# Rope's inverse roots, convolution taps and context sums at new places in a two-block transformer kernel

## What is computed

```python
def mixer(h, ...):
    qa, ka, va, ub, qc, kc, vc, gates = jnp.split(h @ w_in, IN_SPLITS, axis=-1)
    qa = apply_rope(rms_norm(qa.reshape(B, S, 2 * DA_HEADS, DA_HEAD_DIM), qn_g), cos, sin)
    ka = apply_rope(rms_norm(ka.reshape(B, S, 2 * DA_HEADS, DA_HEAD_DIM), kn_g), cos, sin)
    y_a = diff_attention(qa, ka, va, lam, lambda_init, subln_g) @ w_proj_a
    y_b = conformer_conv(ub, w_dw, b_dw, conv_ln_g, conv_ln_b) @ w_proj_b + b_proj_b
    y_c = stick_breaking(qc, kc, vc) @ w_proj_c
    g = jax.nn.sigmoid(gates.reshape(B, S, N_BRANCH, D_MODEL))
    return (g[:, :, 0] * y_a + g[:, :, 1] * y_b + g[:, :, 2] * y_c) @ w_out

def rms_norm(x, g):
    return x * lax.rsqrt(jnp.mean(x * x, axis=-1, keepdims=True) + EPS) * g
# conformer_conv: a * sigmoid(gate), causal depthwise convolution with 31 taps on 512 channels,
# layer norm, silu. The context: ctx is normalised with rms_norm before it meets its weights.
```

## Time and profile before

| | before |
|---|---|
| median of 3 runs | 2458.14 us (2457.7 to 2459.05) |
| span of the profiled execution | 2460.3 us |
| busy PE, DVE, ACT, POOL | 2325.7, 847.0, 568.7, 122.0 us |
| moved by DMA | 673.22 MB, mean 274 GB/s |

### The profile page before, as it was taken

One profiled execution on the slowest core, in us unless ns is written; L12 is line 12 of the kernel. 1 busy time (PEld: TensorE's weight loads), 2 busy tenths in 40 slices (PEclk: granted clock), 3 DMA queues, 4 the chain that ended last, 5 costly groups with the idle time before them and its releaser, 6 DMA issues.

```text
span 2460.3 us, 34607 instructions
## 1 busy us (share of the span) xinstructions
PE 2325.7 (95%) x14027; PEld 1664.9 (68%) x14027; DVE 847.0 (34%) x2149; ACT 568.7 (23%) x1227; POOL 122.0 (5%) x179
## 2 busy tenths in 40 slices
PE   7998999999998987999999999998988999999998
PEld 4857887666665654767896666665646787754764
DVE  0477633222111211396623222121212644421264
ACT  2233412111111112124312111111113433321254
POOL 4010000000000000010000000000000000001110
PEclk9999999999999998999999999999988999999999
DMA  9783594999999995943676999999994254240400
GB/s 338 261 323 108 209 377 163 384 414 414 415 417 412 417 414 186 345 172 139 244 308 245 386 413 414 414 414 417 413 368 144 99 179 149 78 146 32 156 1 18
DMA packets 206907, 673.22 MB, mean 274 GB/s; under 512 B 14000, under 2 KB 74648, under 8 KB 156816
## 3 DMA queue, kind: packets, MB, share of 16 engines
q1 hardware_dynamic: 200064, 656.87, 69.2%
q0 software_dynamic: 6240, 13.99, 1.7%
q10 hardware_dynamic: 432, 0.01, 0.0%
HBM read 661.38 MB, written 9.45 MB: 273 GB/s over the span
## 4 chain that ended last, share of the span: by engine, by line
PE 80%; DMA 11%; DVE 4%; ACT 2%; SPq 1%; issue 1%; ACTq 0%; POOL 0%; DVEq 0%
PE ps L278 45%; PE ps L2168 11%; PE ps L2203 6%; DMA ring<-in_w 6%; DMA ar<-in_w 5%; PE ps L2219 3%; PE ps L1750 2%; PE ps L1198 1%; PE ps L686 1%; PE ps L2851 1%; PE ps L3464 1%; SPq L570 1%; DVE ar L1337 1%; DMA ring<-in_w_in 1%; PE ps L1115 1%
## 5 line engine op out<-in xcount | busy, mean ns | idle before, releaser
L278 PE MATMUL ps<-hT,ring 128*128 128x256 f32 (+2 forms) x2352 | 548.2, 389 | 3.2 <-ACT ar L1566 1.9
L278 PEld LDWEIGHTS ps<-hT,ring 128*128 128x128 f32 (+1 forms) x2352 | 443.8, 192 | 102.2 <-issue 37.6
L2168 PE MATMUL ps<-ring,ar 128*32 128x256 f32 (+2 forms) x2752 | 315.7, 391 | 36.4 <-DMA ring<-in_w 29.3
L2168 PEld LDWEIGHTS ps<-ring,ar 128*32 128x32 f32 (+2 forms) x2752 | 192.0, 125 | 146.2 <-issue 52.6
L2168 PE MATMUL ps<-ar 128*64 128x256 f32 (+2 forms) x1104 | 206.6, 399 | 12.7 <-DMA ar<-in_w 11.3
L2486 DVE SCALAR_TENSOR_TENSOR exact_parts<-ps,ar,exact_parts 128x512 fp32r<-128x512 f32 x100 | 75.1, 751 | 252.9 <-ACT exact_parts L2331 247.3
L2203 PE MATMUL ps<-ring,ar 128*32 128x512 f32 (+2 forms) x680 | 150.1, 625 | 6.8 <-DMA ring<-in_w 6.8
L2168 PEld LDWEIGHTS ps<-ar 128*64 128x64 f32 (+2 forms) x1104 | 120.1, 135 | 37.5 <-issue 15.8
L2462 DVE TENSOR_TENSOR ar<-ar,ps 128x256 f32<-128x256 f32 x50 | 21.1, 421 | 359.5 <-PE ps L2168 359.5
L278 PE MATMUL ps<-ring,ar 128*128 128x512 f32 x320 | 139.8, 593 | 0.9 <-DVE ar L3693 0.9
L2331 ACT ACTIVATE exact_parts<-ps,ar 128x512 fp32r<-128x512 f32 x100 | 68.8, 688 | 243.2 <-PE ps L2203 225.2
(11 more groups left out here) (467 smaller groups left out, 2884.0 us busy)
## 6 DMA issues: line engine op xcount, KB each, us to landing
ring<-in_w SPq DMA_DIRECT2D x257, 1024.0 KB, 17.9
ar<-in_w SPq DMA_DIRECT2D x104, 1024.0 KB, 20.1
ring<-in_w_mod SPq DMA_DIRECT2D x36, 2048.0 KB, 12.1
ring<-in_w_in SPq DMA_DIRECT2D x28, 2048.0 KB, 11.8
ring<-in_ab_w_in SPq DMA_DIRECT2D x47, 1024.0 KB, 11.0
cst<-in_w SPq DMA_DIRECT2D x23, 1024.0 KB, 17.0
ring<-in_w_out SPq DMA_DIRECT2D x4, 2048.0 KB, 10.3
ring<-in_ab_w_out SPq DMA_DIRECT2D x2, 4096.0 KB, 13.4
```

Of the source, the lines that this page charges most:

```text
L278: ins = te.matmul(o, l, r, start=(first and i == 0), stop=(last and i == len(pairs) - 1), skip_group_check=lax)
L2168: ins = te.matmul(b[cols, 0:256], K.x_b[:, kk, in_pair(p, cols)], w[r][:, kk, :], start=(kk == 0), stop=(kk == 7))
```

## The change

Four edits, in both layers unless said otherwise:

- Rope's inverse root. DVE's two steps (L1370, L1373) and ACT's square root go. ACT reads PE's sums itself, with Ln (scale 1/64, bias eps) and then Exp with scale -0.5. The table of both is loaded ahead of rope, and the load at the start of the branches goes.
- The taps. 17 instead of 9 stand behind each turn of rope, so all 124 stand in the projections; `dve_conv_end` pauses for eleven rounds.
- The context sums (layer 0) stand between ACT's evictions of kc and vc instead of behind the last eviction.
- The transfer of the context tokens stands ahead of the transfers of the weights of kc and vc (`in`, 0, 3) instead of behind them.

```diff
+            if (l, b) == (0, 3):
+                K.plan(("ctx",), 1, [(lambda f: f.rearrange("p (i d) -> p i d", i=2),
+                                      I["ctx_2"][0].rearrange("(i p) d -> p i d", p=P))], (K.cst_place, []))
             for q in range(2):
                 cols(("in", l, b, q), I["w_in"][l], b * D + q * 512, 512, 2)
                 for key in early_at(l, after[q]):
                     mod(*key)
-        if l == 0:
-            K.plan(("ctx",), 1, [(lambda f: f.rearrange("p (i d) -> p i d", i=2),
-                                  I["ctx_2"][0].rearrange("(i p) d -> p i d", p=P))], (K.cst_place, []))
...
     yield from act_mod_early(K, l, "qc")
+    ac.preload_act_table_set(LN_EXP)
     for it in range(4):
...
-        ac.wait_ge(*(yield ("q_inv", l, it)))
-        ac.activation(K.q_r[it % 2], K.q_r[it % 2], ACT.Sqrt).then_inc(*K.act("q_rstd", l, it))
+        r = K.q_r[it % 2]
+        ac.wait_ge(*(yield ("q_ss", l, it)))
+        if it >= 2:
+            ac.wait_ge(*(yield ("rope", l, it - 2)))
+        ac.activation(r, K.ps["q_ss", l, it][:, :].rearrange("p (c t) -> p c t", c=2), ACT.Ln, bias=C(K, "eps"),
+                      scale=1.0 / 64).then_inc(*K.act("q_var", l, it))
+        ac.wait_ge(*K.act.all())
+        ac.activation(r, r, ACT.Exp, scale=-0.5).then_inc(*K.act("q_rstd", l, it))
...
+    if l == 0:
+        yield from act_ctx_sums(K)
     for i in range(2):
         ac.wait_ge(*(yield ("vc_ps", l, i)))
         ac.activation(K.vc[:, i, :], K.ps["vc_ps", l, i][:, :], ACT.Copy).then_inc(*K.act("vc", l, i))
     yield from act_mod_early(K, l, "vc")
-    if l == 0:
-        yield from act_ctx_sums(K)
...
-        ve.wait_ge(*(yield ("q_ss", l, it)))
-        ve.tensor_scalar(r, K.ps["q_ss", l, it][:, :].rearrange("p (c t) -> p c t", c=2), 1.0 / 64, EPS, ALU.mult,
-                         ALU.add).then_inc(*K.dve("q_var", l, it))
-        ve.wait_ge(*own())
-        ve.reciprocal(r, r).then_inc(*K.dve("q_inv", l, it))
...
-        dve_conv(K, l, at, at + 9)
-        at += 9
+        dve_conv(K, l, at, at + 17)
+        at += 17
...
 def dve_conv_end(K, l):
     ve = K.ve
-    for n in range(92, 124, 4):
-        dve_conv(K, l, n, n + 4)
-        yield PAUSE
-    yield from pause(3)
+    yield from pause(11)
...
 def act_branches(K, l):
     K.ac.wait_ge(*(yield ("rope", l, 3)))
-    K.ac.preload_act_table_set(LN_EXP)
```

## The result

| | before | after |
|---|---|---|
| median | 2457.92 us (2453.11 to 2459.05, 4 runs) | 2426.70 us (2425.22 to 2428.25, 4 runs) |
| ratio | | 0.9875, 95% interval 0.9861 to 0.9889 |
| span of the profiled execution | 2460.3 us | 2425.3 us |
| busy PE, DVE, ACT, POOL | 2325.7, 847.0, 568.7, 122.0 us | 2311.0, 814.7, 569.8, 135.9 us |

The account below looks back on a forecast made before the run. PE was taken to bound the kernel, waiting for DVE and ACT in the branches. Layer 0's 16.4 us plus layer 1's 9.9, less 0.6, gave 25.7 us off 2458.14: 2432.4 us, range 2429 to 2443.

Parts of the forecast that it names:

- What bounds it, and the gaps: Branches of both layers: PE bounds the kernel and waits there for DVE or ACT, 10.66 us in layer 0, 7.33 in layer 1.
- The rivals that lose the gain to the transfers: Expert stages: weight transfers take half the gain (2445.3 us, chance 0.07) or all of it (2458 us, chance 0.04).
- The inverse root: Rope: DVE loses about 4.0 us a turn, ACT takes Ln at 0.7 and Exp at 0.63 us; nothing on PE's path.
- The rival of a slow pair: Rope's turns: Ln and Exp on ACT hold PE up beyond some 6 us a pair; 2470 us at 8 us, chance 0.03.
- The taps: Projections: taps end 0.5 us later, at 166.6 in layer 0, ahead of PE's first scores; the counted branch gaps should close.
- the 0.4 us of the forecast: Branches, ahead of the convolution's sum: the bank it needs is ready only 0.4 us before PE asks.
- the walk through the rounds: Branches: going through the rounds with the taps out, the convolution's sum is the tightest place, yet all counted gaps should close.
- The clock: Behind long gaps in the branches: slow clock costs PE 2.9 and 2.8 us in layer 0, 2.6 in layer 1.
- The context: Layer 0 branches: weights for the first transposes ready 5.6 us earlier, so PE no longer waits 4.72 us.
- The 0.6 us taken off for slowed taps: Last 45 taps of layer 0: POOL's context passes beside them slow DVE, costing PE 0.6 us, range 0 to 1.5.
- The sum: Both branch stages: 16.4 us in layer 0 plus 9.9 in layer 1, less 0.6, gives 25.7 us; nothing is late next.
- The range: Whole kernel: 2429 us (no slowed tap, the 0.78 us gap gone, scatter of 1.4) to 2443 us; 0.86 inside.

Follow-up runs that it names:

- The half-way kernel: The changed kernel with 16 of the 32 moved taps back in the branches, four in each of the first four rounds; 2435.15 us, ratio 0.9914.
- the run with one tensor input: The changed kernel with the last 45 taps of layer 0 reading one SBUF tensor instead of two, so not accumulated; ratio 0.9869.
- the run that puts it back: The changed kernel with eight DVE instructions of one column more, two behind each rope turn of layer 0, their results unused; 2429.76 us, ratio 0.9893.
- filling: The changed kernel with four products of a constant put into each of three PE waits of 2.23 us; 2419.16 us, ratio 0.9854.

## Why the prediction was wrong, step by step

**What bounds it, and the gaps.** Right. All eight gaps that the sum counted went; the one of 0.78 us ahead of the stage in layer 1, which it left out, stayed. The rivals that lose the gain to the transfers did not come: the experts' legs changed by 0.7 us in one layer and -1.2 in the other.

**The inverse root.** Right: Ln took 0.69 us where 0.7 was taken, Exp 0.63. The rival of a slow pair never came near.

**The taps.** Right: the end at 166.78 us stands against a forecast of 166.6. The gap ahead of the convolution's sum closed in both layers, but with less to spare than the 0.4 us of the forecast. ACT's eviction of the gate product (below, in layer 0) ended at 196.59, and the sum began at 196.67; in layer 1 it was 1091.93 and 1092.02. That the last gap closed whole was luck in part. The half-way kernel shows why the walk through the rounds could be trusted: it gives back the first three gaps at their old sizes and not the fourth.

```profile
196.21 0.38 ACT L1700 ACTIVATE xT<-ps 128x256 f32<-128x256 f32 x1 [0.25 <-PE ps L278]
```

**The clock.** Right in size behind the convolution's sums: 2.79 and 2.57 us against 2.8 and 2.6. Inside the stretches the sum was short by 1.2 us in layer 0 (14.76 against 13.56) and 1.1 in layer 1 (8.42 against 7.33), because I priced a gap at its length; a stop costs PE about 0.3 us beyond it, and there were four in each layer.

**The context.** It had no term of its own, but the prediction let it carry the gap of 4.72 us. It is worth 6.1 us alone, 9.6 beside the taps and 4.9 beside the root, and nothing beside both, so in the changed kernel it carries nothing. That step was wrong and cost the sum nothing, because the other two close the gap.

**POOL beside the taps.** The 0.6 us taken off for slowed taps were wrong, because it was the other engine that paid: not one tap was slowed (17.90 us for 45 are 0.398 each), and POOL took 16.0 us in place of 5.7, which nobody on PE's path waited for. The Trainium skill (SBUF — State Buffer, section "SBUF: two separate sides") says that whichever of the two starts first holds the shared ports for its whole instruction and that the other fully blocks. The traces agree with it in one direction: POOL's first instruction ended only 2.7 us behind the last tap, and the run with one tensor input agrees with the condition of two inputs, as far as POOL is held off. In the other direction they agree in part. In the kernel before, DVE's step at 179.35 began 0.13 us behind the start of POOL's second instruction and took 1.12 us, where the same step took 0.35 at 190.8: it lost 0.8 us and not POOL's 2.84, and the taps behind it kept their length beside the same instruction. The prediction had both rows and drew on the taps.

**The sum, which is the step that failed.** It has terms for the two branch stages and none for the rest of the program, with the words that nothing is late next and PE runs its own queue. At the boundary of the layers the eight DVE instructions fewer moved a stop of 2.9 us out of the critical additions. That is worth 4.5 us by the run that puts it back (10.08 to 14.60), and 4.7 to 5.9 against the traces of before. With the 2.3 us of the stops' restarts and the 0.6 us for the taps, the terms missed by 2.3 + 0.6 + 5.9 = 8.8 us between the two traces; 35.0 us were gained between them and 25.7 forecast, and the remaining 0.5 us lie in the other legs. The medians show 5.5 us of miss, because the first trace of before was a long one (2460.3 us of span, against 2452.8 in the second). Without the boundary's 4.5 to 5.9 us the time would have been 2431.2 to 2432.6 us, inside the range; the changed kernel with the stop put back measured 2429.76, just inside it.

**The range** was wrong at its lower end for the same reason: it took in a slowed tap less, the gap of 0.78 us and a measurement's scatter, but no gain from a place that the change does not touch. The row was there to be seen: "issue" with 2.9 us ahead of seven of the eight additions that the next norm hangs on.

## What to carry to other kernels

When an engine is late in one stage and has no time in the stage before, moving work there and freeing time there are one edit, not two: each alone gave 4 and 8 us here, both 31 (the 8 and the 31 with the boundary's 5 in them). Two edits that close the same gap don't add, so try the large pair before the third. Before trusting a sum, look in the trace for stops named "issue" ahead of critical instructions, since an edit that changes an engine's instruction count may move them, for better or worse: one of the three kinds seen here moved on DVE, the other two stayed.

## What the runs showed of the hardware

- A stop of 2.9 us on DVE and one of 5.2 us on PE with nothing to wait for. The first comes and goes with eight instructions of 128 x 1 elements more or fewer ahead of it. It costs 4.5 to 5.9 us: PE waits 3.4 to 3.8 us instead of 0.5, and its sum behind that runs at a granted clock of 0.54 to 0.71 and takes 5.2 to 6.7 us instead of 3.7.
- POOL's pass of two instructions over 128x1024 took 5.7 us beside the branches, 6.7 beside taps with one tensor input and 16.0 beside taps with two. The taps with two kept their 0.398 us and held POOL off until they ended; of those with one, four took 1.25 us instead of 0.40.
- Behind a wait of 2.23 us the granted clock is sometimes 0.68 over the next 5.3 us (its first 3.3 us at the 1.2 GHz level) and sometimes full, in the same kernel. Behind a wait of 0.51 us after filling it was full at all three places.
- A product of 256 columns in fp32 from a constant takes 0.45 us, recorded as two passes.
